# Retention's values with channels on the partitions, and the head's norm summed across partitions

## What is computed

```
scores = jnp.einsum("bnchd,bnkhd->bnhck", qc, kc) * d_inner
o_inner = jnp.einsum("bnhck,bnkhv->bnchv", scores, vc)
...
def head_group_norm(o, g):
    of = o.astype(jnp.float32)
    mu = jnp.mean(of, axis=-1, keepdims=True)
    var = jnp.mean(jnp.square(of - mu), axis=-1, keepdims=True)
    y = (of - mu) * lax.rsqrt(var + LN_EPS)
    bsz, seq, heads, dv = o.shape
    return (y.reshape(bsz, seq, heads * dv) * g.astype(jnp.float32)).astype(o.dtype)
...
    o = head_group_norm(chunk_retention(q, k, v), ret_gn_g)
    y_a = (jax.nn.silu(g_ret) * o) @ w_ret_out
```

## Time and profile before

| | |
|---|---|
| median of 3 runs | 2086.16 us (2086.12 to 2088.02) |
| the profiled execution's own time | 2087.74 us |
| its span in the profile | 2085.9 us |
| PE busy | 2067.2 us (99%) |
| DVE busy | 1666.1 us (80%) |
| ACT busy | 1058.4 us (51%) |
| POOL busy | 256.7 us (12%) |
| granted TensorE clock, mean | 0.997 |
| DMA | 174 GB/s on average, 361.95 MB |

### The profile page before, as it was taken

How to read it: one execution, slowest core, us unless ns; L and a number is a source line. 1 busy time by engine, 2 the same in 40 slices (tenths; PEclk the granted TensorE clock), 3 DMA queues, 4 the chain that set the end, 5 groups by cost and what they waited for, 6 DMA issues and landing times.

```text
span 2085.9 us, 38628 instructions
## 1 busy us (share of the span) xinstructions
PE 2067.2 (99%) x16378; PEld 2016.3 (97%) x16378; DVE 1666.1 (80%) x2449; ACT 1058.4 (51%) x1282; POOL 256.7 (12%) x176
## 2 busy tenths in 40 slices
PE   9999999999999999999999999999999999999998
PEld 9999999999999999989999999999988999989998
DVE  8987888788769778898986768768698996748765
ACT  6886444457744435355545445434346445445432
POOL 0112055000004510001201001100000301000100
PEclk9999999999999999999999999999999999999999
DMA  7663544563325455443555434445554454534542
GB/s 263 197 205 144 184 182 172 179 216 142 122 102 193 160 188 214 172 181 142 199 186 175 169 142 176 176 165 212 182 182 142 182 185 181 182 131 174 196 144 104
DMA packets 58300, 361.95 MB, mean 174 GB/s; under 512 B 6736, under 2 KB 9360, under 8 KB 21136
## 3 DMA queue, kind: packets, MB, share of 16 engines
q1 hardware_dynamic: 58128, 359.48, 48.4%
HBM read 358.37 MB, written 1.08 MB: 172 GB/s over the span
## 4 chain that ended last, share of the span: by engine, by line
PE 94%; DVE 3%; ACT 1%; issue 1%; POOL 0%; DMA 0%; SPq 0%; DVEq 0%; ACTq 0%
PE acc L639 77%; PE acc L638 7%; PE acc L756 1%; PE acc L755 1%; PE acc L754 1%; DVE w_lo L1192 1%; PE acc L959 1%; ACT w_hi L2059 1%; PE pA L1008 1%; PE pC L802 0%; PE pB L1032 0%; PE pB L1119 0%; PE pD L1119 0%; PE pB L1094 0%; PE pA L1094 0%
## 5 line engine op out<-in xcount | busy, mean ns | idle before, releaser
L639 PE MATMUL acc<-in_hi,w_hi 128*128 128x256 f32 x4656 | 1306.7, 286 | 6.5 <-DVE in_hi L1280 3.8
L639 PE MATMUL acc<-in_hi,w_lo 128*128 128x256 f32 x4656 | 1295.8, 284 | 0.1
L639 PE MATMUL acc<-in_lo,w_hi 128*128 128x256 f32 x4656 | 1233.0, 284 | 0.0
L2059 ACT CAST w_hi<-raw 128x2048 fp32r<-128x2048 f32 (+1 forms) x341 | 615.4, 1805 | 634.8 <-PE acc L639 541.2
L1192 DVE TENSOR_TENSOR w_lo<-raw,w_hi 128x2048 fp32r<-128x2048 f32 (+1 forms) x341 | 739.5, 2169 | 229.3 <-ACT w_hi L2059 228.3
L639 PEld LDWEIGHTS acc<-in_hi,w_hi 128*128 128x128 f32 x4656 | 894.2, 192 | 10.0 <-DVE in_hi L1280 4.0
L639 PEld LDWEIGHTS acc<-in_hi,w_lo 128*128 128x128 f32 x4656 | 894.2, 192 | 0.6 <-DVE w_lo L1524 0.3
L639 PEld LDWEIGHTS acc<-in_lo,w_hi 128*128 128x128 f32 x4656 | 856.7, 192 | 1.2 <-issue 1.0
L2663 POOL TENSOR_TENSOR in_lo<-arena,in_hi 128x256 fp32r<-128x256 f32 (+1 forms) x112 | 139.0, 1241 | 1202.4 <-ACT in_hi L2521 509.9
L1839 DVE SCALAR_TENSOR_TENSOR arena<-arena,cols 128x256 f32<-128x256 f32 x480 | 200.3, 487 | 0.0
L2673 POOL TENSOR_TENSOR arena<-arena 128x256 f32<-128x256 f32 x44 | 84.7, 1925 | 393.0 <-ACT arena L2343 393.0
(11 more groups left out here) (293 smaller groups left out, 1629.3 us busy)
## 6 DMA issues: line engine op xcount, KB each, us to landing
raw<-in_wide SPq DMA_DIRECT2D x285, 1024.0 KB, 4.8
raw<-in_narrow SPq DMA_DIRECT2D x64, 704.0 KB, 4.0
arena<-cs_rows SPq DMA_DIRECT2D x16, 256.0 KB, 4.6
arena<-in_mem SPq DMA_DIRECT2D x3, 1024.0 KB, 4.8
x<-in_x SPq DMA_DIRECT2D x4, 256.0 KB, 6.2
raw<-in_wide SPq DMA_DIRECT2D x2, 512.0 KB, 5.8
tables<-in_tables SPq DMA_DIRECT2D x1, 1024.0 KB, 14.9
arena<-cs_rows SPq DMA_DIRECT2D x16, 64.0 KB, 5.6
```

What stands on the lines that cost most here:

```text
L639: return mm(outs[m], w[:, k, at], moving[:, c, :], start=start, stop=stop)
L2059: copy(w_hi[s][:, 0:n], raw[g % RAW][:, 0:n]).then_inc(hi_ready, 1)
```

## The change

`ret_values` exchanges stationary and moving operand: the values (`rv_tok`) are the weights and the scores move, so that 128 channels stand on the partitions and 256 positions on the free axis, for four channel chunks in banks pC and pD. ScalarE (`ret_out_of`) squares both banks into `rv_tok`, which is no longer needed, and copies the banks, times the gain, to `ret_o`, which is where `ret_y` lies. VectorE adds the squares of the four chunks (`ret_sums`); TensorE sums across the partitions with two products of one column each (`ret_stat`); ScalarE takes the root (`ret_std`), VectorE the reciprocal (`ret_root`), TensorE spreads it over the partitions by two products with the identity (`ret_back`), and VectorE multiplies the head by it in place (`ret_normed`, 128x1024). `ret_gate` becomes one product of 128x512 in SBUF, and `ret_turn` is gone.

```
@@ -299,7 +299,7 @@
         rt = view(13296, 4, T)
         ang = view(8192, 4, T)
         ret_s = view(13296, 2, 2, T)
-        o_tok = [view(1024 * h, 2, TT, T) for h in range(RH)]
+        ret_o = [view(1024 * h, 4, T) for h in range(RH)]
         ln_sq = view(8192, DC, T)
 
         x_q = view(0, DC, T)
@@ -1016,21 +1020,34 @@
                 pe.wait_ge(v_mid, n + 1)
                 if n:
                     pe.wait_ge(ro_a, n)
-                vs = slice(h * RV, (h + 1) * RV)
-                mm(pC[:], r_s[:, h % 2, 0:P], rv_tok[:, 0, vs], start=True, stop=True)
-                mm(pD[:], r_s[:, h % 2, P:T], rv_tok[:, 0, vs], start=True, stop=False)
-                mm(pD[:], r_s[:, h % 2, T:T + P], rv_tok[:, 1, vs], start=False, stop=True).then_inc(ro_mm, 1)
-
-            def ret_turn(l, u):
-
-                h, p = divmod(u, 2)
-                pe.wait_ge(ro_a, RH * l + h + 1)
-                if 8 * l + u:
-                    pe.wait_ge(gated_v, 8 * l + u)
-                for c in range(2):
-                    for t in range(TT):
-                        last = transpose(pB[:, c * T + t * P:c * T + (t + 1) * P], o_tok[h][:, p, t, c * P:(c + 1) * P], ident[:])
-                last.then_inc(rt_mm, 1)
+                for c in range(RV // P):
+                    at, out = h * RV + c * P, c % 2 * T
+                    bk = (pC, pD)[c // 2]
+                    mm(bk[:, out:out + T], rv_tok[:, 0, at:at + P], r_s[:, h % 2, 0:T], start=True, stop=False)
+                    last = mm(bk[:, out + P:out + T], rv_tok[:, 1, at:at + P], r_s[:, h % 2, T:T + P], start=False, stop=True)
+                last.then_inc(ro_mm, 1)
+
+            def ret_stat(l, h):
+
+                n = RH * l + h
+                pe.wait_ge(rsum_v, n + 1)
+                if n:
+                    pe.wait_ge(rscale_v, n - (h == RH - 1))
+                for t in range(TT):
+                    last = mm(pB[:, 2 * T - 8 + 2 * h + t:2 * T - 7 + 2 * h + t], rv_tok[:, 0, h * RV + t * P:h * RV + (t + 1) * P],
+                              ones[:, 0:1], start=True, stop=True)
+                last.then_inc(rst_mm, 1)
+
+            def ret_back(l, h):
+
+                n = RH * l + h
+                pe.wait_ge(rrec_v, n + 1 + (h == RH - 2))
+                if n:
+                    pe.wait_ge(rscale_v, n)
+                for t in range(TT):
+                    last = mm(pB[:, t * P:(t + 1) * P], small[:, 2 * h + t:2 * h + t + 1].broadcast_to([P, P]), ident[:],
+                              start=True, stop=True)
+                last.then_inc(rback_mm, 1)
 
             def mixer(l):
                 def run():
@@ -1047,14 +1064,20 @@
                             ret_scores(l, j // 2)
                         elif j >= 3:
                             ret_values(l, j // 2 - 1)
+                        if j in (4, 6):
+                            ret_stat(l, j // 2 - 2)
+                        if j in (5, 7):
+                            ret_back(l, j // 2 - 2)
                     project("ret_v", after=scores_and_values)
                     _, gate_unit, _ = units("ret_g")
                     for u in range(8):
                         gate_unit(u, u)
                         if u == 0:
                             ret_values(l, RH - 1)
-                        else:
-                            ret_turn(l, u - 1)
+                        if u < 2:
+                            ret_stat(l, 2 + u)
+                        elif u < 4:
+                            ret_back(l, u)
                     def conv_mean(u, j):
                         if j == 3:
                             pe.wait_ge(ln_sum, 2 * l + 1)
@@ -1062,7 +1085,7 @@
                         if j == 6:
                             pe.wait_ge(ln_sum, 2 * l + 2)
                             mm(pA[:, T:2 * T], ones[:], ln_sq[:, 0, :], start=True, stop=True).then_inc(lnv_mm, 1)
-                    project("gates", after=lambda u, j: ret_turn(l, 7) if j == 0 else None)
+                    project("gates")
                     E.wait(gin_ready, 8)
                     project("ret_out", after=conv_mean)
                     E.wait(in_ready, NORM_PIECES)
@@ -1850,17 +1873,30 @@
 
                 n = RH * l + h
                 dve.wait_ge(rstd_a, n + 1)
-                recip(small[:, 14:16], small[:, 12:14]).then_inc(rrec_v, 1)
+                recip(small[:, 2 * h:2 * h + 2], small[:, 2 * h:2 * h + 2]).then_inc(rrec_v, 1)
+
+            def ret_sums(l, h):
+
+                n = RH * l + h
+                dve.wait_ge(rsq_a, n + 1)
+                squares = rv_tok[:, :, h * RV:(h + 1) * RV]
+                E.mark(tt(squares[:, 0, :], squares[:, 0, :], squares[:, 1, :], ALU.add))
+                E.settle()
+                tt(squares[:, 0, 0:T], squares[:, 0, 0:T], squares[:, 0, T:2 * T], ALU.add).then_inc(rsum_v, 1)
+
+            def ret_normed(l, h):
+
+                n = RH * l + h
+                dve.wait_ge(rback_mm, n + 1)
+                dve.wait_ge(ro_a, n + 1)
+                tt(ret_o[h], ret_o[h], pB[:, 0:T].unsqueeze(1).broadcast_to([P, 4, T]), ALU.mult).then_inc(rscale_v, 1)
 
             def ret_gate(l, u):
 
-                n = 8 * l + u
-                dve.wait_ge(rt_mm, n + 1)
                 dve.wait_ge(acc_free, [t.base for t in segs if t.name == "ret_g"][l] + u + 1)
-                for c in range(2):
-                    ins = stt(out=ret_y[:, 2 * u + c, :], in0=pB[:, c * T:(c + 1) * T], scalar=wcol(f"ret_gain{l}", 2 * u + c),
-                              in1=ret_s[:, u % 2, c, :], op0=ALU.mult, op1=ALU.mult)
-                    E.mark(ins) if c == 0 else ins.then_inc(gated_v, 1)
+                dve.wait_ge(rscale_v, RH * l + u // 2 + 1)
+                y = ret_y[:, 2 * u:2 * u + 2, :]
+                tt(y, y, ret_s[:, u % 2], ALU.mult).then_inc(gated_v, 1)
 
             def ret_gated(u, j, banks):
                 y = gate[:, bass.ds(u, 1), :]
@@ -1891,22 +1927,27 @@
                         project(n, rotary, lambda u, j, banks: conv_tap(l, u // 2 + o) if j % 2 == 0 else None, early=True)
 
                     def values(u, j, banks):
-                        if j in (4, 6):
-                            ret_root(l, j // 2 - 2)
                         tap = 4 + j + (j > 3) + (j > 5)
-                        conv_tap(l, tap, (lambda: ret_root(l, 2)) if j == 7 else None)
+                        if j in (5, 7):
+                            ret_normed(l, j // 2 - 2)
+                        conv_tap(l, tap, (lambda: ret_sums(l, j // 2 - 1)) if j in (3, 5, 7) else
+                                 (lambda: ret_root(l, j // 2 - 2)) if j in (4, 6) else None)
                         if j in (3, 5):
                             conv_tap(l, tap + 1)
                         if j % 2 == 0:
                             ret_decay(l, j // 2)
                     project("ret_v", None, values)
 
+                    def roots_of(l):
+                        ret_root(l, 2)
+                        ret_root(l, 3)
+
                     def gated(u, j, banks):
-                        if j == 1:
-                            ret_root(l, 3)
+                        if j in (2, 3):
+                            ret_normed(l, j)
                         if j:
                             ret_gate(l, u - 1)
-                        conv_tap(l, j + 14)
+                        conv_tap(l, j + 14, (lambda: ret_sums(l, 3)) if j == 0 else (lambda: roots_of(l)) if j == 1 else None)
                     project("ret_g", None, gated)
 
                     def last_gated(u, j, banks):
@@ -2482,30 +2523,29 @@
                         E.mark(fn(v[0], v[0], ACT.Identity, bias=small[:, 8:9]))
                         fn(v[1], v[1], ACT.Identity, bias=small[:, 9:10]).then_inc(v_mid, 1)
                         if j >= 3:
-                            ret_std(l, h - 1)
+                            ret_out_of(l, h - 1)
                     elif j >= 4:
-                        ret_scaled(l, h - 2)
+                        ret_std(l, h - 2)
                 return use
 
-            def ret_std(l, h):
+            def ret_out_of(l, h):
 
                 n = RH * l + h
                 act.wait_ge(ro_mm, n + 1)
-                if n:
-                    act.wait_ge(rrec_v, n)
-                junk = o_tok[h].rearrange("p a t n -> p (a t n)")
-                for t, bk in enumerate((pC, pD)):
-                    E.mark(fn(junk[:, t * RV:(t + 1) * RV], bk[:], ACT.Square, accum_out=small[:, 10 + t:11 + t]))
-                E.settle()
-                fn(small[:, 12:14], small[:, 10:12], ACT.Sqrt, bias=wcol("eps_ln"), scale=1.0 / RV).then_inc(rstd_a, 1)
-
-            def ret_scaled(l, h):
+                for i, bk in enumerate((pC, pD)):
+                    ins = fn(rv_tok[:, i, h * RV:(h + 1) * RV], bk[:], ACT.Square)
+                    E.mark(ins) if i == 0 else ins.then_inc(rsq_a, 1)
+                for c in range(RV // P):
```

(34 more changed lines are left out.)

2 lines of the change are left out of this document (removed).

## The result

| | before | changed |
|---|---|---|
| median of 20 runs each | 2086.64 us | 2090.90 us |
| profiled execution: time, span | 2087.74, 2085.9 us | 2091.68, 2089.9 us |
| ratio to before | | 1.0020, 95% interval 1.0014 to 1.0026 |
| stretch of the first layer, of the second | 173.47, 173.48 us | 175.45, 175.46 us |

The forecast was 2089.2 us in 2085.5 to 2092.0; 2090.90 lies in the part above 2090.3 to which the prediction gave 0.24. The *stretch* is the measure of all that follows: from the first product of `ret_scores` of a layer to the end of the product behind o3, read from PE's timeline. It doesn't vary with what comes ahead of the mixer, as a run's time does. Two stretches are 3.96 us longer, and the span is 4.0 longer: the whole difference lies there.

The account below looks back on a forecast made before the run. PE was taken to bound the kernel, with DVE gapless from g1 on. Per layer -0.42 + 0.4 + 1.6 = +1.6 us, +3.2 for two layers on 2086.16, stated as 2089.2 us; range 2085.5 to 2092.0.

Parts of the forecast that it names:

- PE's own work: TensorE per layer: sums and spreads add 3.44 us, turns save 3.86, values cost the same; -0.42 us.
- wait of head 2's spread: Behind g2, PE waits for the last two reciprocals, which come in the middle of g1's tap; 0.4 us per layer.
- DVE late at t3 to t5 and behind: PE waits about 1.6 us per layer at t3 and t4 for DVE's remainder (`w_lo`).
- six pieces at 1.05: Between g1's body and t4's remainder, six of POOL's pieces each cost DVE 1.05 us, the gate waiting like a tap.
- first rival: The gate does not wait for POOL, so the wait at t4 is gone: 2086.1 us; chance 0.25.
- second rival: DVE falls further behind at t3 to t5, `ret_normed` waiting for POOL; the product behind o3 joins: 2093.6 us; chance 0.12.

Follow-up runs that it names:

- run 5: Changed kernel without 7 of 8 channels of body g4's convolution tap, reciprocals ahead of the gate; 2086.43 us (one run), stretches 173.32 and 173.32 us.
- run 4: Changed kernel without 7 of 8 channels of the convolution tap in body g4; 2088.78 us, stretches 174.10 and 174.11 us.
- run 12: Changed kernel with one sum-and-spread product per head, POOL's low parts on DVE, taps a body ahead from g0 to g5; 2084.04 us.
- run 1: Changed kernel with the two reciprocals of heads 2 and 3 moved ahead of the gate; 2093.38 us, stretches 175.59 and 177.07 us.
- run 9: Changed kernel with POOL's pieces for the gate units cut to one column; 2090.01 us (one run), stretches 174.10 and 174.10 us.
- runs 2 and 10: 2: changed kernel with the silu in banks pC and pD, 2089.27 us; 10: also the gate in halves and reciprocals first, 2089.34 us.
- run 11: Changed kernel with POOL's eight low parts of the gate units per layer on DVE, reciprocals first; 2088.59 us, stretches 174.03 and 174.02 us.
- run 6: Changed kernel with the tap of body g1 issued in body g0, reciprocals ahead of the gate; 2091.72 us, stretches 177.09 and 175.61 us.
- run 7: Changed kernel with one product per head for sum and spread, ScalarE making 1/sqrt; 2095.14 us (one run), stretches 177.19 and 177.17 us.
- run 8: Changed kernel with one sum-and-spread product per head, silu in banks and the early tap; 2091.98 us, stretches 175.37 and 175.79 us.

## Why the prediction was right

| term, us per layer | predicted | measured | by |
|---|---|---|---|
| PE's own work | -0.42 | -0.15 | run 5 against before |
| wait of head 2's spread | +0.4 | +0.78 | run 4 less run 5 |
| DVE late at t3 to t5 and behind | +1.6 | +1.35 | changed less run 4 |
| sum | +1.6 | +1.98 | the stretches |

The three terms are off by +0.27, +0.38 and -0.25, which partly cancel: that the sum came as near as it did is in part luck. Of the 1.7 us between forecast and median, 0.9 lie in the stretches (3.96 where 3.04 was forecast), 0.5 in the base (2086.64 where the forecast built on 2086.16), and 0.3 outside both.

- **PE's work.** The 3.86 us of turns went. Values cost 2.62 and not 2.57 (915.05 to 917.67 for head 0), 0.2 per layer; spreads 0.45 and not 0.43. One column does cost what more do: a pair of one-column products 0.44 with the 0.10 in the unit behind it, the single product of 256 columns in run 12 0.43. The 60 cycles of the Trainium skill (TensorE: Matmul & The Clock Gate, section Back-to-back issue gap) are not what this form costs: 0.11 us per instruction. They are the matmul's gap by itself; the same section says that in a stream of weight loads and matmuls both set the distance, and these products each have a weight load of their own.
- **Head 2's spread.** Place and cause were right, the size was half. It came 0.3 us later than worked out (970.46 against 970.15), and behind the 0.52 of waiting the products took 0.71 instead of 0.45. That restart had no term.
- **DVE late.** The 1.6 was booked at t3 and t4. There PE loses 0.44; 0.42 more stands ahead of t5, 0.23 in the seven units behind it (behind the stall of run 1 too, 46.31 us for eight units instead of 46.08), and 0.26 behind o3, which I had given to a rival only: 1.35 in all. Why they are there was right in the main: POOL's pieces at 1.05 each, without which run 9 has none of these waits. Two things were wrong in the working. I let the gate absorb them; in the changed kernel it never grew (0.68), and the taps behind it did, the pieces being held out through the gate. And six pieces at 1.05 ahead of t4's remainder became five: the sixth fell behind it (4.29 from 1023.47), and so t5's was the last to be late.
- **That the three terms add** was an unspoken step, and held only for the sum. Run 1 shows that the second can't be won back while the third is there.
- **The first rival** (gate indifferent, 2086.1) needed a gate that lets POOL in cheaply. In runs 2 and 10 it has its bank operand again and brings back only part: a piece that meets the gate costs 0.45 and 0.39 instead of 1.04, against 0.25 before, and others miss the gate. So the operand alone doesn't do it. Why in the kernel before seven pieces cost 0.25 each is not shown; the timing of POOL's requests is a candidate that no run tries alone.
- **The second rival** fell: `ret_normed` took 1.21 us everywhere, as a reader of a bank.

## What to carry to other kernels

Where two engines of near equal load work side by side, a wait on one may be covered by the lateness of the other: take work off the late one first, then measure what the wait is worth. Ask of each instruction on VectorE not only how long it takes but whether it keeps GpSimd out, and what GpSimd then stands beside; here, handing VectorE the eight pieces at 0.60 us each was cheaper than having it wait for them (run 11). Work moved into idle time counts only if the next step does not wait for somebody else anyway.

## What the hardware showed that I had not expected

- **A stall on PE can cost its clock.** In run 1 PE stands 2.03 us in both layers, ahead of 1023.35 and of 1665.18. The windows behind the two stalls (busy time of PE, PEld, DVE, ACT, POOL, granted clock, DMA share, GB/s):

```profile
1023.40:1029.20 5.80, 5.80 (x49) 5.80 (x50) 5.80 (x11) 0.64 (x2) 0.00 (x0) 1.00 0.49 181
1665.10:1670.90 5.80, 5.72 (x35) 5.75 (x36) 5.80 (x11) 0.76 (x3) 0.00 (x0) 0.71 0.47 181
```

  Behind the second the mean granted clock is 0.71, part of the time at 1.2 instead of 2.4 GHz: 35 matmuls instead of 49, and the second stretch is 177.07 against 175.59. The same happened in the first layers of run 6 and run 7, behind stalls of 2.03 and 2.10 us (0.71 each). It did not happen in their second layers, behind 2.05 us (run 6), 2.07 and 2.08 us (run 7), nor in the first layer of run 8 behind 1.5 us (1.00 each). A stall of 2 us so cost either 2 or about 3.5, three times in seven the latter; what decides is left open.
- **POOL waits for DVE even with a one-column piece.** In run 9 such a piece lasts from 987.25 to 990.18, 2.93 us, and the taps beside it take their 3.25:

```profile
987.25 2.93 POOL L2704 TENSOR_TENSOR in_lo<-arena,in_hi 128x2 fp32r<-128x2 f32 x1 [4.78 <-ACT in_hi L2561]
```

- **Who gets in is not regular.** In the changed kernel the piece from 991.95 came in amid taps and was done in 1.30 us. The one from 1005.42 also asked amid taps (those from 1004.06, which still took only 3.25 us) and was held out through the subtraction until the gate was over (1010.04). I have no run that tells why.
